# A two-layer decoder step on one core: rectifier and squares regrouped over the engines, and a row spread made with three bf16 pieces

## The chip, the core and the metric

The kernel runs on one core of a Trainium2 chip. The core has a matrix engine (TensorE, PE in the profile; its weight loads are shown apart as PEld), a vector engine (VectorE, DVE), a scalar engine (ScalarE, ACT), a general engine (GpSimd, POOL) and a queue engine that issues transfers (SyncE, SP). The metric is the device time of one execution in microseconds, and the number compared is the median of several executions.

## What is computed

One inference step over 1024 prompt tokens and 32 sample tokens (8 sequences of 4), 1056 columns in all, through two layers. The first layer's mixer is a stabilised matrix-memory recurrence (mLSTM) over 8 heads, evaluated in chunks of 128 tokens; the second's is attention over a paged cache. Both layers end in a squared-ReLU MLP of width 4096. The two pieces that the change touches:

```python
# first mixer, per head and chunk of 128 tokens
b = cumsum(lf); m_inter = b + m
m_t = maximum(m_inter, max(log_d)); w_inter = exp(m_inter - m_t)
s = (q @ k.T) * exp(log_d - m_t)          # log_d = b_t - b_s + ig_s where s <= t
num = w_inter * (q @ C) + s @ v
# MLP, in both layers
u = rmsnorm(h, norm_mlp) @ w_up
h = h + square(relu(u)) @ w_down
```

## The kernel before, in words

Activations lie transposed: features on the partitions, the 1056 tokens as columns, cut into NT = 3 tiles of TW = 352. Every dense product is made of three matmuls on pairs of reduced-precision parts (high by high, high by low, low by high: L212 to L214, and L812 to L814 in the first mixer), so each activation and each weight must exist as a `hi` part and a `lo` part. Weights come in panels of 128 x 1024: SyncE loads one (`w_raw`), GpSimd casts it to `w_hi` (L162) and subtracts to get `w_lo` (L164), and TensorE uses it for three tiles. Two panels are in flight; GpSimd may begin on a buffer once the tiles that read its old contents are done (`tile_ready`). All orders are written out by hand, one program per engine, with counting semaphores between them.

**MLP (`out_and_mlp`).** Eight chunks of 512 hidden features in each layer, 16 in all. A chunk has four `up` panels (u = 0..3), each with three tiles of 24 matmuls, so 12 tiles n = 0..11, and then the `down` product, whose first panel reads, for token tile t, what was made of all four up tiles of t. Each up tile goes through five instructions before `down` can read it: ACT takes it from the accumulator bank with Relu (L2085, which frees the bank, `tile_free`), DVE multiplies by the inverse rms (L2133), ACT squares (L2087), DVE casts the square to `u_hi` (L2135), DVE subtracts `u_hi` from the square to get `u_lo` (L2137, `u_ready`). TensorE's only wait for this, beside the banks, stands at the start of `down` (`u_ready`). The accumulations into `h` in the down part are L2143.

**First mixer (`mixer_a`).** Before the heads can be worked on, a chain on rows of 8 partitions (one per head) x 1056 tokens makes the gate sums `ub` (= b - m, in `squares`) and `winter` (= w_inter), on DVE and ACT in turn, while TensorE makes the first projection tiles; DVE takes those tiles from the banks in the same in-order stream (`read_out`), and TensorE has two banks for them. Then the heads go in four pairs, p = 0..3. For each pair TensorE has to copy a head's row over all 128 partitions. It does so with a small matmul whose stationary operand picks the row: `spread` makes `ub` rows for the decay weights (L850, 512 columns, four per pair, with a bf16 mask added by L852; a small one for the sample tokens at L857), `w_inter` makes `winter` rows for the queries (L866, 352 columns, three per pair, stationary operand `sel`, "p_pair_rows"). Both have f32 operands with 8 rows. The profile shows each such matmul as two records. Between them stand thirds of the next pair's projection tiles, so that TensorE always has work. ACT turns each spread into decay weights (`decay`, L1012, `dec_ready`), and the next spread waits for it since there is one bank. In pairs p > 0 ACT's stream has, between the first and the second decay, the inverse norm of the pair before (`inverse_rms`, L1072 and L1074), which waits for a chain of small DVE instructions (`sums`, L1265 to L1274).

Of the kernel before, what the change touches and what calls it, by code (L numbers as in the profile page):

```python
# [17 lines left out]
ALU = mybir.AluOpType  # L18
# [4 lines left out]
BF16 = mybir.dt.bfloat16  # L23
# [597 lines left out]
def mixer_a(nc, m, own):  # L621
# [7 lines left out]
    FIRST_TILES = 3 * NT + 3  # L629

# [57 lines left out]
    with ExitStack() as c:  # L688
# [13 lines left out]
        pick, sel = sb("pick_gates", [P, P]), sb("pair_rows", [40, HP, P])  # L702
# [4 lines left out]
        graw, y, ub, winter = m.sq[0], m.sq[1], m.acc, m.acc[32:32 + HA, :]  # L707
# [9 lines left out]
        chain, achain, picked = own.sem("dve_step"), own.sem("act_step"), own.sem("gates_picked")  # L717
        y_ready, sp_ready, m_ready, we_in, stack_act = own.sem("softplus_in"), own.sem("softplus_out"), own.sem("m_ready"), own.sem("w_inter_in"), own.sem("stack_act")
# [53 lines left out]
        def _(pool):  # L772
# [17 lines left out]
            heads = m.ident[32:32 + HA, 32:32 + HA].rearrange("r (p h) -> r p h", h=2)  # L790
            pool.tensor_copy(sel[32:32 + HA, :, :].rearrange("r p (h e) -> r p h e", h=2),
                             heads.unsqueeze(3).broadcast_to([HA, HP, 2, DK])).then_inc(filled, 1)
            pool.wait_ge(filled, 12)
# [4 lines left out]
        def _(pe):  # L798
# [43 lines left out]
            def spread(x):  # L842
# [5 lines left out]
                if j < 2:  # L848
                    head = 2 * p + h2
                    pe.matmul(m.bank[2][:, :], m.ident[0:HA, head:head + 1].broadcast_to([HA, P]), ub[0:HA, 512 * j:512 * j + 512],  # L850
                              start=True, stop=False)
                    last = pe.matmul(m.bank[2][:, :], m.identb[:, :], m.causal[:, :].unsqueeze(1).broadcast_to([P, 4, P]),  # L852
                                     start=False, stop=True)
                else:
                    for h2 in range(2):
                        head, z = 2 * p + h2, m.bank[2][0:NS, h2 * NS:(h2 + 1) * NS]
                        pe.matmul(z, m.ident[0:HA, head:head + 1].broadcast_to([HA, NS]), ub[0:HA, SEQ:T], start=True, stop=False)  # L857
# [75 lines left out]
            pe.wait_ge(filled, 12)  # L933
# [16 lines left out]
            pe.wait_ge(col_ready, 5)  # L950
            for p in range(HP + 1):
# [19 lines left out]
        def _(act):  # L971
# [8 lines left out]

            act.wait_ge(y_ready, 1)
# [5 lines left out]
            act.activation(winter, bsum, ACT.Exp).then_inc(stack_act, 1)  # L987
            for g, (b0, nb) in enumerate(GROUPS):
# [123 lines left out]
        def _(dve):  # L1112
# [35 lines left out]
            dve.wait_ge(filled, 12)  # L1148
# [43 lines left out]
            read_out(TAU0 + 5)  # L1192
            dve.wait_ge(stack_act, 2)
# [1055 lines left out]
```

## Time and profile before

| | before |
|---|---|
| median of 3 runs | 3019.81 us (3016.09 to 3023.21) |
| the profiled execution, its own time | 3017.92 us |
| the profiled execution, span of the records | 3016.1 us |
| TensorE matmul busy | 2879.8 us, 95% |
| TensorE weight load busy | 2622.8 us, 87% |
| VectorE busy | 1368.9 us, 45% |
| ScalarE busy | 821.7 us, 27% |
| GpSimd busy | 741.8 us, 25% |
| mean granted TensorE clock | 0.981 of full speed |

The span is the time from the first to the last record of one execution, and what lies around it is 1.8 us. Busy shares are means over stages that differ; how TensorE's idle time and its slots are spent in the two stages in question is in the rows further down. A matmul's own duration includes its way through the array and overlaps with the next: what it takes of TensorE's time is read from the distance of starts.

### The profile page before, as it was taken

The numbers are of one execution on the slowest core, as the hardware profiler recorded it, in microseconds if no ns is written. First come the engines' busy times: TensorE is split into PE (matmuls) and PEld (weight loads), VectorE is DVE, ScalarE is ACT, GpSimd is POOL, SyncE is SP. The second block draws the span as 40 slices with busy tenths as digits, with TensorE's granted clock in tenths as the row PEclk, the third lists the DMA queues.
The fourth block names the chain that finished last, engine by engine and source line by source line (L and its number), as shares of the span: only waits on it lengthen the run. The fifth ranks groups of instructions, "written<-read, shape, count | busy, mean of one in ns | idle before, by whom it ended". The sixth has DMA issues, their size and how long they took to land. (4 is left out here: it accounts for less than half of the span.)

```text
span 3016.1 us, 49373 instructions
## 1 busy us (share of the span) xinstructions
PE 2879.8 (95%) x19749; PEld 2622.8 (87%) x19749; DVE 1368.9 (45%) x2039; ACT 821.7 (27%) x1661; POOL 741.8 (25%) x450
## 2 busy tenths in 40 slices
PE   7999997999999999998999999998799999999998
PEld 6889887999999999996776677665699999999998
DVE  6223345444433344354556655564544443334434
ACT  4121123211110011124555655555321111011112
POOL 3221112223232323232122111210123232323231
PEclk8999998999999999999999999998899999999999
DMA  5575524223232232324443443434311111111112
GB/s 165 182 138 192 99 30 94 84 85 90 91 93 88 85 96 83 98 86 123 116 127 99 120 117 109 123 94 116 127 42 49 43 49 42 44 47 42 49 42 78
DMA packets 361448, 277.24 MB, mean 92 GB/s; under 512 B 31378, under 2 KB 352914, under 8 KB 359250
## 3 DMA queue, kind: packets, MB, share of 16 engines
q1 hardware_dynamic: 340074, 261.97, 29.8%
q10 hardware_dynamic: 21224, 13.15, 2.3%
q8 instruction: 108, 1.77, 0.2%
q14 instruction: 42, 0.34, 0.0%
HBM read 251.06 MB, written 91.11 MB: 113 GB/s over the span
## 5 line engine op out<-in xcount | busy, mean ns | idle before, releaser
L162 POOL CAST w_hi<-w_raw 128x1024 fp32r<-128x1024 f32 x193 | 206.9, 1072 | 1628.1 <-PE bank L214 902.9
L212 PE MATMUL bank<-p_u_hi,w_hi 128*128 128x352 f32 x1536 | 496.8, 323 | 16.0 <-DVE p_u_lo L2137 14.6
L212 PE MATMUL bank<-x_hi,w_hi 128*128 128x352 f32 x1536 | 495.6, 323 | 1.7 <-PEq L2227 1.7
L213 PE MATMUL bank<-p_u_lo,w_hi 128*128 128x352 f32 x1536 | 495.6, 323 | 0.0
L214 PE MATMUL bank<-p_u_hi,w_lo 128*128 128x352 f32 x1536 | 495.4, 323 | 0.0
L214 PE MATMUL bank<-x_hi,w_lo 128*128 128x352 f32 x1536 | 493.5, 321 | 0.0
L213 PE MATMUL bank<-x_lo,w_hi 128*128 128x352 f32 x1536 | 492.9, 321 | 0.0
L164 POOL TENSOR_TENSOR w_lo<-w_raw,w_hi 128x1024 fp32r<-128x1024 f32 x193 | 477.1, 2472 | 15.5
L2143 DVE TENSOR_TENSOR h<-bank,h 128x352 f32<-128x352 f32 x384 | 199.0, 524 | 466.5 <-PE bank L214 466.5
L2085 ACT ACTIVATE p_relu<-bank 128x352 f32<-128x352 f32 x192 | 89.3, 465 | 1039.2 <-PE bank L214 1033.0
L212 PEld LDWEIGHTS bank<-p_u_hi,w_hi 128*128 128x128 f32 x1536 | 288.5, 188 | 20.9 <-issue 18.7
L1886 DVE TENSOR_TENSOR_SCAN square<-square,zero 128x512 f32<-128x512 f32 (+5 forms) x192 | 214.9, 1134 | 167.8 <-ACT square L1746 166.6
L212 PEld LDWEIGHTS bank<-x_hi,w_hi 128*128 128x128 f32 x1536 | 288.1, 188 | 2.8 <-issue 2.8
L213 PEld LDWEIGHTS bank<-x_lo,w_hi 128*128 128x128 f32 x1536 | 289.0, 188 | 0.0
L214 PEld LDWEIGHTS bank<-p_u_hi,w_lo 128*128 128x128 f32 x1536 | 288.7, 188 | 0.0
L213 PEld LDWEIGHTS bank<-p_u_lo,w_hi 128*128 128x128 f32 x1536 | 288.6, 188 | 0.0
L214 PEld LDWEIGHTS bank<-x_hi,w_lo 128*128 128x128 f32 x1536 | 288.4, 188 | 0.0
L2133 DVE TENSOR_TENSOR p_relu<-p_relu,rms_inverse 128x352 f32<-128x352 f32 x192 | 133.3, 694 | 275.4 <-ACT p_relu L2085 275.4
L2135 DVE CAST p_u_hi<-p_relu_sq 128x352 fp32r<-128x352 f32 x192 | 163.2, 850 | 108.4 <-ACT p_relu_sq L2087 108.4
L812 PE MATMUL bank<-x_hi,w_hi 128*128 128x352 f32 x576 | 200.9, 349 | 4.3 <-DVE p_v_next L1138 2.3
L814 PE MATMUL bank<-x_hi,w_lo 128*128 128x352 f32 x576 | 186.8, 324 | 0.0
L813 PE MATMUL bank<-x_lo,w_hi 128*128 128x352 f32 x576 | 186.5, 324 | 0.0
(259 smaller groups left out, 4560.9 us busy)
## 6 DMA issues: line engine op xcount, KB each, us to landing
k_pages<-in_cache_k SPq DMA_DIRECT2D x64, 512.0 KB, 6.2
w_raw<-in_w_up SPq DMA_DIRECT2D x64, 512.0 KB, 4.1
v_pages<-in_cache_v SPq DMA_DIRECT2D x64, 512.0 KB, 4.6
w_raw<-in_w_down SPq DMA_DIRECT2D x64, 512.0 KB, 3.4
p_pages<-k_pages SPq DMA_DIRECT2D x256, 128.0 KB, 2.4
p_pages<-v_pages SPq DMA_DIRECT2D x256, 128.0 KB, 2.4
w_raw<-in_w_in_a SPq DMA_DIRECT2D x25, 512.0 KB, 3.9
h_spill<-h SPq DMA_DIRECT2D x16, 528.0 KB, 5.4
```

The source lines that it names most:

```text
L162: pool.tensor_copy(m.whi[slot][:, :], m.wraw[slot][:, :]).then_inc(w.hi, 1)
L164: pool.tensor_tensor(m.wlo[slot][:, :], m.wraw[slot][:, :], f32(m.whi[slot][:, :]), ALU.subtract)\
L212: pe.matmul(bank[:, 0:TW], wh, xh, start=(k == 0), stop=False)
L213: pe.matmul(bank[:, 0:TW], wh, xl, start=False, stop=False)
L214: last = pe.matmul(bank[:, 0:TW], wl, xh, start=False, stop=(k == nk - 1))
L812: pe.matmul(bank[:, 0:TW], wh, xh, start=(kk == 0), stop=False)
L813: pe.matmul(bank[:, 0:TW], wh, xl, start=False, stop=False)
L814: last = pe.matmul(bank[:, 0:TW], wl, xh, start=False, stop=(kk == KT - 1))
L1886: dve.tensor_tensor_scan(stick, stick, m.zero[:, 0:1].broadcast_to([P, hi - lo]), sticks[h2][:, hi:hi + 1] if x else 1.0, ALU.mult, ALU.ad ...
L2133: dve.tensor_tensor(relu[t][:, :], relu[t][:, :], m.rs[:, toks], ALU.mult).then_inc(scaled, 1)
L2135: dve.tensor_copy(uhi[:, u, toks], sqr[t][:, :]).then_inc(hi_ready, 1)
L2143: dve.tensor_tensor(ht, m.bank[t][:, 0:TW], ht, ALU.add).then_inc(w.tile_free[t], 1)
```

## The change

In the MLP, DVE makes the scaled rectifier in one instruction from the bank (max with 0, times the inverse rms), which now frees the bank. ACT makes both squares from its result, first the one that is written as `u_hi`, then the f32 one. DVE only subtracts. In the first mixer, `ub` and `winter` are each split into three bf16 pieces that add up to the f32 value, at partitions 0, 32 and 64 of a 72-row tensor, and the picking matrices are bf16 with ones at the three places, so that a spread is one bf16 matmul with 72 rows. ACT clears and fills these tensors at the mixer's start, and ACT and DVE make the pieces in turn. GpSimd no longer fills the f32 `sel`.

```diff
+        u3, w3 = own.tensor("u_pieces", [PIECES, T], BF16), own.tensor("w_inter_pieces", [PIECES, T], BF16)
+        of_head, of_pair = own.tensor("head_rows", [PIECES, HA, P], BF16), own.tensor("pair_rows", [PIECES, HP, P], BF16)
...
-                    pe.matmul(m.bank[2][:, :], m.ident[0:HA, head:head + 1].broadcast_to([HA, P]), ub[0:HA, 512 * j:512 * j + 512],
-                              start=True, stop=False)
+                    pe.matmul(m.bank[2][:, :], of_head[:, head, :], u3[:, 512 * j:512 * j + 512], start=True, stop=False)
...
-                pe.matmul(m.bank[7][:, 0:TW], sel[32:32 + HA, p, :], winter[:, x * TW:(x + 1) * TW], start=True, stop=True).then_inc(wsp_ready, 1)
+                pe.matmul(m.bank[7][:, 0:TW], of_pair[:, p, :], w3[:, x * TW:(x + 1) * TW], start=True, stop=True).then_inc(wsp_ready, 1)
...
             pe.wait_ge(col_ready, 5)
+            pe.wait_ge(piece, 4)
+            pe.wait_ge(rest_ready, 4)
...
+            for tile in (u3[:, :], w3[:, :], of_head[:, :, :].rearrange("r h e -> r (h e)"), of_pair[:, :, :].rearrange("r p e -> r (p e)")):
+                step(act.copy(tile, m.zero[0:PIECES, 0:1].broadcast_to([PIECES, tile.shape[-1]])))
+            for r in (0, 32, 64):
+                rows_, heads = slice(r, r + HA), m.identb[r:r + HA, r:r + HA]
+                step(act.copy(of_head[rows_, :, :], heads.unsqueeze(2).broadcast_to([HA, HA, P])))
+                step(act.copy(of_pair[rows_, :, :].rearrange("r p (h e) -> r p h e", h=2),
+                              heads.rearrange("r (p h) -> r p h", h=2).unsqueeze(3).broadcast_to([HA, HP, 2, DK])))
...
+            act.copy(u3[0:HA, :], ub[0:HA, :]).then_inc(piece, 1)
+            act.wait_ge(stack_act, 2)
+            act.copy(w3[32:32 + HA, :], winter).then_inc(piece, 1)
+            act.wait_ge(rest_ready, 1)
+            act.copy(u3[32:32 + HA, :], rest[32:32 + HA, :]).then_inc(piece, 1)
+            act.wait_ge(rest_ready, 2)
+            act.copy(w3[64:64 + HA, :], rest[64:64 + HA, :]).then_inc(piece, 1)
...
             read_out(TAU0 + 5)
+            dve.wait_ge(piece, 1)
+            dve.tensor_tensor(rest[32:32 + HA, :], ub[0:HA, :], u3[0:HA, :], ALU.subtract).then_inc(rest_ready, 1)
             dve.wait_ge(stack_act, 2)
...
             step(dve.memset(num[:, :, :, :], 0.0))
-            for e in range(6, FIRST_TILES):
+            read_out(TAU0 + 6)
+
+            dve.wait_ge(piece, 2)
+            dve.tensor_tensor(rest[64:64 + HA, :], winter, w3[32:32 + HA, :], ALU.subtract).then_inc(rest_ready, 1)
+            dve.wait_ge(piece, 3)
+            dve.wait_ge(rest_ready, 2)
+            dve.tensor_tensor(u3[64:64 + HA, :], rest[32:32 + HA, :], u3[32:32 + HA, :], ALU.subtract).then_inc(rest_ready, 1)
+            read_out(TAU0 + 7)
+            dve.wait_ge(piece, 4)
+            dve.tensor_tensor(w3[0:HA, :], rest[64:64 + HA, :], w3[64:64 + HA, :], ALU.subtract).then_inc(rest_ready, 1)
+            for e in range(8, FIRST_TILES):
                 read_out(TAU0 + e)
...
-                        act.wait_ge(w.tile_ready, i * TILES_C + (TILES_OUT + n + 1))
-                        act.activation(relu[t][:, :], m.bank[t][:, 0:TW], ACT.Relu).then_inc(w.tile_free[t], 1)
-                        act.wait_ge(scaled, i * (UT * NT) + (n + 1))
+                        toks = slice(t * TW, (t + 1) * TW)
+
+                        act.wait_ge(w.tile_free[t], i * USES_C + (USES_OUT + u + 1))
+                        act.activation(uhi[:, u, toks], relu[t][:, :], ACT.Square)
                         act.activation(sqr[t][:, :], relu[t][:, :], ACT.Square).then_inc(sq_ready, 1)
...
-                        dve.wait_ge(w.tile_free[t], i * USES_C + (USES_OUT + u + 1))
-                        dve.tensor_tensor(relu[t][:, :], relu[t][:, :], m.rs[:, toks], ALU.mult).then_inc(scaled, 1)
+                        dve.wait_ge(w.tile_ready, i * TILES_C + (TILES_OUT + n + 1))
+                        dve.scalar_tensor_tensor(out=relu[t][:, :], in0=m.bank[t][:, 0:TW], scalar=0.0, in1=m.rs[:, toks],
+                                                 op0=ALU.max, op1=ALU.mult).then_inc(w.tile_free[t], 1)
                         dve.wait_ge(sq_ready, i * (UT * NT) + (n + 1))
-                        dve.tensor_copy(uhi[:, u, toks], sqr[t][:, :]).then_inc(hi_ready, 1)
-                        dve.wait_ge(hi_ready, i * (UT * NT) + (n + 1))
                         dve.tensor_tensor(ulo[:, u, toks], sqr[t][:, :], f32(uhi[:, u, toks]), ALU.subtract)\
                             .then_inc(u_ready, 1)
```

**The MLP, one up tile.** VectorE's rows for one tile, before (the semaphore that each waits for stands behind it; `relu_scaled` counts DVE's products, `relu_sq_ready` ACT's squares):

```order
L2133 TENSOR_TENSOR p_relu<-p_relu,rms_inverse 128x352 [waits pw1_tile_free0]
L2134 REGISTER_ALU
L2135 CAST p_u_hi<-p_relu_sq 128x352 [waits p3_relu_sq_ready]
L2137 TENSOR_TENSOR p_u_lo<-p_relu_sq,p_u_hi 128x352 [waits p3_u_hi_ready]
```

and now:

```order
L2163 SCALAR_TENSOR_TENSOR p_relu<-bank,rms_inverse 128x352 [waits pw1_tile_ready]
L2165 ISA
L2166 TENSOR_TENSOR p_u_lo<-p_relu_sq,p_u_hi 128x352 [waits p3_relu_sq_ready]
```

VectorE's first instruction now waits for TensorE's tile itself, and the cast is gone from its stream. ScalarE's rows for the same tile were L2085 (Relu from the bank) and L2087 (Square, after `relu_scaled`); now they are two squares side by side:

```order
L2116 ACTIVATE p_u_hi<-p_relu 128x352 [waits pw1_tile_free0]
L2117 ACTIVATE p_relu_sq<-p_relu 128x352
```

**The mixer's start.** VectorE's stream between the projection tiles TAU0+5 and TAU0+8, before (`p_k<-bank` are the read-outs):

```order
L1138 TENSOR_TENSOR p_v_next<-bank,rms_inverse 128x352 [waits pw0_tile_ready]
L1195 COPY p_w_end<-squares 8x8 [waits p2_stack_act]
L1196 COPY p_w_end<-squares 8x8
L1197 TENSOR_TENSOR p_w_diag<-p_w_end,identity 8x128 [waits p2_dve_step]
L1200 MEMSET p_numerator 128x2322
L1136 SCALAR_TENSOR_TENSOR p_k<-bank,rms_inverse 128x352 [waits pw0_tile_ready,p2_dve_step]
L1136 SCALAR_TENSOR_TENSOR p_k<-bank,rms_inverse 128x352 [waits pw0_tile_ready] x2
```

and now:

```order
L1155 TENSOR_TENSOR p_v_next<-bank,rms_inverse 128x352 [waits pw0_tile_ready]
L1211 TENSOR_TENSOR square<-squares,p_u_pieces 8x1056 [waits p2_piece_made]
L1214 COPY p_w_end<-squares 8x8 [waits p2_stack_act]
L1215 COPY p_w_end<-squares 8x8
L1216 TENSOR_TENSOR p_w_diag<-p_w_end,identity 8x128 [waits p2_dve_step]
L1219 MEMSET p_numerator 128x2322
L1153 SCALAR_TENSOR_TENSOR p_k<-bank,rms_inverse 128x352 [waits pw0_tile_ready,p2_dve_step]
L1223 TENSOR_TENSOR square<-squares,p_w_inter_pieces 8x1056 [waits p2_piece_made]
L1226 TENSOR_TENSOR p_u_pieces<-square,p_u_pieces 8x1056 [waits p2_rest_made,p2_piece_made]
L1153 SCALAR_TENSOR_TENSOR p_k<-bank,rms_inverse 128x352 [waits pw0_tile_ready]
L1229 TENSOR_TENSOR p_w_inter_pieces<-square,p_w_inter_pieces 8x1056 [waits p2_piece_made]
L1153 SCALAR_TENSOR_TENSOR p_k<-bank,rms_inverse 128x352 [waits pw0_tile_ready]
```

Four subtractions of 8x1056 have come in between the read-outs. ScalarE's stream has ten fills (L983 to L987) ahead of its first exponential (L982 before) and four casts behind the exponential of `winter` (L987 before). TensorE's stream keeps its order.

## Rows read from the trace of the kernel before

**Rows 1.** The page's slices: granted TensorE clock, in tenths of full speed.

```profile
PEclk8999998999999999999999999998899999999999
```

**Rows 2.** Who waited for whom on TensorE: us in total, times, longest.

```profile
PE bank L212 <- DVE p_u_lo L2137: 14.6, 16, 0.9
```

**Rows 3.** Timeline, the last up tile of an MLP chunk: start, us, engine, instruction, idle before.

```profile
629.68 0.46 ACT L2085 ACTIVATE p_relu<-bank 128x352 f32<-128x352 f32 x1 [2.26 <-PE bank L214]
...
630.93 2.56 POOL L164 TENSOR_TENSOR w_lo<-w_raw,w_hi 128x1024 fp32r<-128x1024 f32 x1
...
631.26 0.50 ACT L2087 ACTIVATE p_relu_sq<-p_relu 128x352 f32<-128x352 f32 x1 [1.11 <-DVE p_relu L2133]
...
631.79 1.89 DVE L2135 CAST p_u_hi<-p_relu_sq 128x352 fp32r<-128x352 f32 x1 [0.56 <-ACT p_relu_sq L2087]
...
633.72 0.53 DVE L2137 TENSOR_TENSOR p_u_lo<-p_relu_sq,p_u_hi 128x352 fp32r<-128x352 f32 x1
...
634.39 0.40 PE L212 MATMUL bank<-p_u_hi,w_hi 128*128 128x352 f32 x1 [0.89 <-DVE p_u_lo L2137]
```

**Rows 4.** The page's group of the additions into h (mean ns after the busy time).

```profile
L2143 DVE TENSOR_TENSOR h<-bank,h 128x352 f32<-128x352 f32 x384 | 199.0, 524 | 466.5 <-PE bank L214 466.5
```

**Rows 5.** Timeline, another up tile: a subtraction beside GpSimd.

```profile
596.59 2.41 POOL L164 TENSOR_TENSOR w_lo<-w_raw,w_hi 128x1024 fp32r<-128x1024 f32 x1
...
596.74 2.64 DVE L2137 TENSOR_TENSOR p_u_lo<-p_relu_sq,p_u_hi 128x352 fp32r<-128x352 f32 x1
```

**Rows 6.** Timeline of TensorE around the first spread of pair 0.

```profile
101.83 0.32 PE L814 MATMUL bank<-x_hi,w_lo 128*128 128x352 f32 x1
...
102.08 1.12 PE L850 MATMUL bank<-squares,identity 8*128 8x512 f32 x2
...
103.14 0.39 PE L852 MATMUL bank<-causal,identity_bf 128*128 128x512 bf16 x1
...
103.53 0.32 PE L813 MATMUL bank<-x_lo,w_hi 128*128 128x352 f32 x1
...
103.69 0.32 PE L814 MATMUL bank<-x_hi,w_lo 128*128 128x352 f32 x1
```

**Rows 7.** Timeline of TensorE around the first query-weight spread of pair 0.

```profile
122.67 0.32 PE L814 MATMUL bank<-x_hi,w_lo 128*128 128x352 f32 x1
...
122.91 0.85 PE L866 MATMUL bank<-squares,p_pair_rows 8*128 8x352 f32 x2
...
123.96 0.32 PE L813 MATMUL bank<-x_lo,w_hi 128*128 128x352 f32 x1
```

**Rows 8.** Timeline, second decay and third spread of pair 1, and of pair 2.

```profile
209.64 1.12 ACT L1012 ACTIVATE p_decay_weights<-bank,p_gate_columns 128x128 f32<-128x128 f32 x4
...
211.11 1.12 PE L850 MATMUL bank<-squares,identity 8*128 8x512 f32 x2
...
311.91 1.13 ACT L1012 ACTIVATE p_decay_weights<-bank,p_gate_columns 128x128 f32<-128x128 f32 x4
...
314.37 1.12 PE L850 MATMUL bank<-squares,identity 8*128 8x512 f32 x2
```

**Rows 9.** Timeline of the mixer's start: ScalarE, VectorE, GpSimd and TensorE.

```profile
59.89 1.08 ACT L982 ACTIVATE p_states<-p_states 8x1056 f32<-8x1056 f32 x1 [13.37 <-DVE p_states L1156]
...
73.80 1.24 DVE L1183 TENSOR_TENSOR p_decay_weights<-p_numerator,p_states 8x1056 f32<-8x1056 f32 x1
...
78.02 1.09 ACT L987 ACTIVATE squares<-p_states 8x1056 f32<-8x1056 f32 x1 [3.88 <-DVE p_states L1189]
...
78.98 2.40 POOL L164 TENSOR_TENSOR w_lo<-w_raw,w_hi 128x1024 fp32r<-128x1024 f32 x1
...
79.14 2.26 DVE L1195 COPY p_w_end<-squares 8x8 f32<-8x8 f32 x1 [0.72 <-ACT squares L987]
...
84.25 0.52 DVE L1136 SCALAR_TENSOR_TENSOR p_k<-bank,rms_inverse 128x352 f32<-128x352 f32 x1
...
85.13 0.32 PE L812 MATMUL bank<-x_hi,w_hi 128*128 128x352 f32 x1
```

More of the change, by code:

```diff
@@ L629, in mixer_a @@
     FIRST_TILES = 3 * NT + 3
+    PIECES = 2 * 32 + HA
     FILL = {"u": 1, "k": 1, "v": 1, "wsp": 2, "out": 1, "scores": 2, "dc": 3, "dcs": 2, "num": 3}
@@ L701, in mixer_a @@
         ss, den, den2 = sb("head_squares", [P, 2, NB]), sb("denominator", [P, 2, NB]), sb("denominator_sq", [P, 2, NB])
-        pick, sel = sb("pick_gates", [P, P]), sb("pair_rows", [40, HP, P])
+        pick = sb("pick_gates", [P, P])
+        u3, w3 = own.tensor("u_pieces", [PIECES, T], BF16), own.tensor("w_inter_pieces", [PIECES, T], BF16)
+        of_head, of_pair = own.tensor("head_rows", [PIECES, HA, P], BF16), own.tensor("pair_rows", [PIECES, HP, P], BF16)
         gbias, m0, mprev, mend = sb("gate_bias", [40, 1]), sb("m_start", [HA, SB]), sb("m_prev", [HA, 16]), sb("m_end", [HA, 16])
@@ L717, in mixer_a @@
         chain, achain, picked = own.sem("dve_step"), own.sem("act_step"), own.sem("gates_picked")
+        piece, rest_ready = own.sem("piece_made"), own.sem("rest_made")
         y_ready, sp_ready, m_ready, we_in, stack_act = own.sem("softplus_in"), own.sem("softplus_out"), own.sem("m_ready"), own.sem("w_inter_in"), own.sem("stack_act")
@@ L789, in _ @@
             pool.wait_ge(filled, 11)
[L790 to L793, printed above, removed]
             weight_splits(pool, m, w, stages)
@@ L856, in spread @@
                         head, z = 2 * p + h2, m.bank[2][0:NS, h2 * NS:(h2 + 1) * NS]
-                        pe.matmul(z, m.ident[0:HA, head:head + 1].broadcast_to([HA, NS]), ub[0:HA, SEQ:T], start=True, stop=False)
+                        pe.matmul(z, of_head[:, head, 0:NS], u3[:, SEQ:T], start=True, stop=False)
                         last = pe.matmul(z, m.identb[0:NS, 0:NS], m.causal_s[:, :], start=False, stop=True)
@@ L932, in _ @@
             pe.wait_ge(w.tile_free[0], NT)
-            pe.wait_ge(filled, 12)
+            pe.wait_ge(filled, 11)
             for t in range(NT):
@@ L1147, in _ @@
             dve.wait_ge(landed, 64)
-            dve.wait_ge(filled, 12)
+            dve.wait_ge(filled, 11)
             dve.wait_ge(picked, NT)
@@ L1961, in out_and_mlp @@
         h_back = [own.sem(f"h_back{k}") for k in range(KT)]
-        scaled, sq_ready, hi_ready, u_ready = own.sem("relu_scaled"), own.sem("relu_sq_ready"), own.sem("u_hi_ready"), own.sem("u_ready")
+        sq_ready, u_ready = own.sem("relu_sq_ready"), own.sem("u_ready")
         out_v = w_out.rearrange("(k p) (m j) -> m p k j", p=P, j=P)
```

2 lines of the change are left out of this document (1 added, 1 removed).

## The prediction

> **What bounds the kernel now.** I read TensorE's waits first, then the timeline of the two stages that the change touches, and last what the other engines do in them. TensorE is busy nearly all the time, so a microsecond is won only where TensorE itself has less to do, or where it stops to wait. In the MLP it stops once a chunk for `u_lo`: 16 times, 14.6 us in all, 0.9 each [rows 2]. The chain behind one such wait is in [rows 3]. The last up tile is ready at 629.68, where ACT begins; DVE's product, ACT's square (631.26), DVE's cast (631.79, 1.89 us) and DVE's subtraction follow, and the subtraction ends at 634.25. TensorE goes on at 634.39, after 0.89 of waiting. The cast is long because of GpSimd: GpSimd's own subtraction runs from 630.93 to 633.49, and the cast ends 0.19 after it. A DVE instruction that has both inputs in SBUF meets the same fate: in [rows 5] a subtraction that began inside GpSimd's ended 0.38 after it (599.38 against 599.00), 2.64 instead of 0.53. Instructions that read a bank don't: the 384 additions into h, many beside GpSimd, have a mean of 524 ns [rows 4].
>
> In the first mixer TensorE hardly waits, it works. One spread there costs it 1.38: from the start of L814 at 101.83 to that of L813 at 103.53 are 1.70, in which two ordinary matmuls take their 0.16 each (103.53 to 103.69) [rows 6]. One query-weight spread costs 0.97 (122.67 to 123.96, less 0.32) [rows 7].
>
> **MLP.** The change takes out ACT's Relu and DVE's cast, puts DVE's one instruction on the bank, and adds a square on ACT. From 629.68: DVE's instruction 0.53 (a scalar_tensor_tensor from a bank took 0.52 [rows 9]; it has one SBUF input and so is like [rows 4]), to 630.21; two squares of 0.50 [rows 3] with 0.04 for each hand-over, to about 631.28. The subtraction can then start, but GpSimd has been at its own since 630.93. So the stall moves from the cast to the subtraction. GpSimd's lasts 2.40 when no cast comes into it (2.41 in [rows 5], 2.40 in [rows 9], against 2.56 in [rows 3]), to 633.33; 0.38 later, at 633.71, `u_lo` is there, 0.54 before the old 634.25. TensorE's wait falls from 0.89 to 0.35. Over 16 chunks: 8.6 us. Bounds: if GpSimd takes 2.56 all the same, 0.38 a chunk, 6.1 us; if the subtraction isn't held at all, the whole wait goes, 14.2 us. I take 8.6, by the row of the same instruction.
>
> The Trainium skill (SBUF — State Buffer, Who interferes with whom) says that the port DVE and GpSimd share is locked for a whole instruction by whoever starts first, and that a DVE instruction with two SBUF inputs contends with a GpSimd one that reads SBUF. This speaks against counting the full 14.2. Taken literally it is a little harsher than the row: the subtraction would run its whole 0.53 after 633.33, to 633.86, which gives 0.39 a chunk and 6.2 us instead of 8.6.
>
> The added square costs nothing: ACT is done at 631.25 and has its next tile 3.8 us (24 matmuls of 0.16) after this one. The bank is freed at 630.21 instead of 630.14, and TensorE needs it two tiles later. DVE's read-outs queue behind the held subtraction as they did behind the held cast, and come out 0.5 earlier.
>
> **Mixer, what TensorE saves.** The bf16 mask matmul of 512 columns takes 0.23 of TensorE's time (103.14 to 103.53, less one slot of 0.16) [rows 6]. The new spread has that form, with 72 rows instead of 128; I give it 0.23, plus the gap of 0.09 that stands ahead of the f32 one (102.08 less 101.83 less 0.16). The f32 one took 1.38 less 0.23, 1.15. Saved: 0.83, 16 times, 13.3 us. The query-weight spread has 352 columns: 0.16 plus 0.09 against 0.97, saved 0.72, 12 times, 8.7 us. Together 22.0. The four small sample spreads I leave out. Bound: four passes of 0.23 are 0.92, and the f32 spread from 102.08 on took 1.06; if the 0.14 of loads and gaps stays with each of the 28, 3.9 less. On the other side there is no more than the 0.09 of each, 2.5.
>
> **Where a part is given back.** There is one bank for the spreads, so the third waits until ACT has read the second out of it. In pair 1 ACT's second decay ends at 210.76 and the third spread begins at 211.11 [rows 8]. ACT can't be earlier: its stream has the inverse norm of the pair before ahead of that decay, and this waits for DVE's chain of sums, which starts with the last projection tile of the pair before, ahead of the first spread. So the third spread can come forward only by 0.35, less 0.14 of hand-over (634.25 to 634.39 in [rows 3]), where the first two have saved 1.66: 1.45 is lost. Pair 3 has the same distances. In pair 2 the decay ends at 313.04 and the spread begins at 314.37, so 1.19 can be used and 0.47 is lost. Pair 0 has no inverse norm. Given back: 3.4.
>
> **The mixer's start.** ACT's ten fills stand ahead of its first exponential. By width (1.08 for 1056 columns [rows 9]) they come to 1.1, 1.1, 1.05, 0.5 and three times 1.6, with hand-overs about 9 us. The exponential now comes at 59.89 after 13.37 of idle time [rows 9], with only two transfer issues in it, so the fills are hidden; were that cover gone, each microsecond would be one later for the projection tiles behind DVE. Taking the fill of `sel` from GpSimd gives nothing, since its first split there waits for a load.
>
> DVE's four subtractions of 8x1056 are 1.24 each [rows 9]. The first waits for ACT's cast (79.11 plus 1.08, 80.2) and so falls into GpSimd's subtraction (78.98 to 81.38). An instruction so held ends its free time, less 0.15, after GpSimd's end (0.38 for 0.53 in [rows 5]), so it ends at 81.38 less 0.15 plus 1.24, 82.5. The copy that stands behind it was held by the same GpSimd instruction and ended at 81.40. All behind it thus comes 1.1 later: the read-out at 84.25, which ended at 84.77, now ends at 85.9, and the tile for which TensorE needs that bank began at 85.13 and now begins at 86.0. Cost 0.9. The next read-out stands behind two more subtractions (to 88.4, read by 88.9), and TensorE is at its tile until 89.8. All pieces are there by about 91, and the first spread begins at 102.08 [rows 6], 11 us later: the new waits of TensorE cost nothing.
>
> **Sum.** 8.6 plus 22.0 less 3.4 less 0.9 is 26.3. The profiled execution took 3017.92, which leaves 2991.6; the median of the runs shown is 1.9 above it, so about 2993.
>
> **The rivals.**
> *The subtraction gets ahead of GpSimd* (chance 0.12). Then the 0.89 goes whole, 14.2 for 8.6: 2988. It would have to start 0.35 earlier than I find.
> *The third spreads are not held* (0.08). If the chain of sums moves forward with TensorE after all, 3.4 come back: 2990. Against it stands that DVE's chain begins before the first spread.
> *Smaller terms* (0.17). The 0.14 stays with each spread and the MLP gives 6.2: 6.3 less, 3000. What speaks for it is that 72 rows and a changed stationary operand occur in no row.
> *A late start* (0.08). The fills, at four thirds of their price, 12 us, would just fit; if the pieces' exchange or the fills push the first tiles by 3 to 6 us more, 2996 to 3000.
> *The mixer gains nothing* (0.02), since TensorE's gain is all taken by other waits: 8.6 alone, 3011.
> *The clock falls: slower than before* (0.03). The granted clock is the thing that could undo it all. Slices of 75.4 us stand at 8 tenths, which is a part of the slice at 1.2 instead of 2.4 GHz, the others at 9 or more [rows 1]; one such slice costs up to 0.2 times 75.4, 15 us. From two more of them (30 against 26.3) it decides, and the time would be about 3024. The new pauses at the mixer's start (0.9) and at two third spreads (1.5) could do it. Against it: the 16 waits of 0.9 in the MLP left the slices at 9.
> The forecast itself has 0.50.
>
> **How the numbers follow.** The range reaches from the full MLP gain with the 3.5 us by which the runs shown scatter, 2985, to the smaller terms, 3001. It leaves out the dead mixer, the falling clock and the tails of the others, some 0.15. A measurement of this kernel can tell about 0.2%, 6 us. All cases but the last lie more than that below 3019.81, so faster has 0.96, the same 0.01, slower 0.03.
>
> **What would show it.** The wait of L212's successor for `u_lo` at 16 times 0.35, 5 to 6 us in all; the subtraction in the last up tiles at 2.3 to 2.5 us and no longer 0.53, GpSimd's beside it at 2.40; no DVE cast. The spread at one record of about 0.4 and 0.55 from neighbour to neighbour with the mask; a wait or gap of 1.4 ahead of the third spread of pairs 1 and 3; the first read-out of `k` about 1.1 later against its tile. I am wrong if the subtraction has 0.53 there, if the 72-row matmul is slow, or if the clock's slices show new eights.

## The result, and the profile after

The changed kernel takes 2979.27 us (median of 4 runs, 2977.72 to 2984.09), beside 3017.95 (3015.16 to 3023.21) for the kernel before: ratio 0.9878, 95% interval [0.9861, 0.9894]. The forecast was 2993, with a range down to 2985: right in sign and close in the two stages that it took apart, 12 us too little in all. The profiled execution took 2977.9 us.

The page of the changed kernel, busy time and the granted clock by slices:

```profile
PE 2847.8 (96%) x19713; PEld 2609.5 (88%) x19713; DVE 1303.7 (44%) x1851; ACT 819.4 (28%) x1675; POOL 731.6 (25%) x449
...
PEclk9999998999999999999999999999899999999999
```

TensorE has 36 records fewer (19749 before), and two slices fewer at 8 tenths than in [rows 1].

**MLP.** The timeline around the last up tile of a chunk (start, us, engine, instruction, idle before), and the wait's row of the waits of TensorE:

```profile
610.95 0.53 DVE L2163 SCALAR_TENSOR_TENSOR p_relu<-bank,rms_inverse 128x352 f32<-128x352 f32 x1 [1.81 <-PE bank L214]
...
611.51 0.50 ACT L2116 ACTIVATE p_u_hi<-p_relu 128x352 fp32r<-128x352 f32 x1 [2.93 <-DVE p_relu L2163]
...
611.91 0.48 ACT L2117 ACTIVATE p_relu_sq<-p_relu 128x352 f32<-128x352 f32 x1
...
612.20 2.40 POOL L164 TENSOR_TENSOR w_lo<-w_raw,w_hi 128x1024 fp32r<-128x1024 f32 x1
...
612.43 2.55 DVE L2166 TENSOR_TENSOR p_u_lo<-p_relu_sq,p_u_hi 128x352 fp32r<-128x352 f32 x1 [0.95 <-ACT p_relu_sq L2117]
...
614.44 0.32 PE L214 MATMUL bank<-p_u_hi,w_lo 128*128 128x352 f32 x1
...
615.13 0.40 PE L212 MATMUL bank<-p_u_hi,w_hi 128*128 128x352 f32 x1 [0.36 <-DVE p_u_lo L2166]
615.37 0.32 PE L213 MATMUL bank<-p_u_lo,w_hi 128*128 128x352 f32 x1
```

```profile
PE bank L212 <- DVE p_u_lo L2166: 5.8, 16, 0.4
```

This is the picture of [rows 3] with one engine's turn less. GpSimd takes its undisturbed 2.40; the subtraction that began 0.23 later lasts 2.55 instead of 0.53 and ends at 614.98, 0.38 after GpSimd. The wait is 0.36, where [rows 2] have 0.9.

**First mixer.** A spread with its mask, and a query-weight spread, each with a neighbour:

```profile
102.75 0.32 PE L814 MATMUL bank<-x_hi,w_lo 128*128 128x352 f32 x1
102.91 0.39 PE L850 MATMUL bank<-p_u_pieces,p_head_rows 72*128 72x512 bf16 x1
103.14 0.38 PE L851 MATMUL bank<-causal,identity_bf 128*128 128x512 bf16 x1
103.17 0.51 PE L812 MATMUL bank<-x_hi,w_hi 128*128 128x352 f32 x1
103.52 0.32 PE L813 MATMUL bank<-x_lo,w_hi 128*128 128x352 f32 x1
...
120.06 0.32 PE L814 MATMUL bank<-x_hi,w_lo 128*128 128x352 f32 x1
120.22 0.32 PE L865 MATMUL bank<-p_w_inter_pieces,p_pair_rows 72*128 72x352 bf16 x1
120.26 0.45 PE L812 MATMUL bank<-x_hi,w_hi 128*128 128x352 f32 x1
120.54 0.32 PE L813 MATMUL bank<-x_lo,w_hi 128*128 128x352 f32 x1
```

From L814 to L813 are 0.77 less two slots of 0.16: 0.45 for a spread and its mask, for 1.38 in [rows 6]. The other costs 0.48 less 0.32, 0.16, for 0.97 in [rows 7]. The pair of small sample spreads went the other way: with their masks they cost 0.67 (116.55 to 117.54, less 0.32) for 0.48 before (119.34 to 120.14), four times, 0.8 us in all. What is given back: the third spread of pair 1 (timeline), and TensorE's waits in the first mixer:

```profile
204.13 0.31 ACT L1089 ACTIVATE p_head_squares<-p_head_squares,eps 128x18 f32<-128x18 f32 x1 [3.92 <-DVE p_head_squares L1303]
...
204.60 1.12 ACT L1029 ACTIVATE p_decay_weights<-bank,p_gate_columns 128x128 f32<-128x128 f32 x4
...
205.78 0.39 PE L850 MATMUL bank<-p_u_pieces,p_head_rows 72*128 72x512 bf16 x1 [1.46 <-ACT p_decay_weights L1029]
```

```profile
PE bank L850 <- ACT p_decay_weights L1029: 3.5, 3, 1.5
PE bank L812 <- DVE p_k L1153: 0.9, 1, 0.9
```

The first of these rows holds three waits: 1.46 in pair 1 and 1.46 in pair 3, each of the third spread for the second decay, and 0.56 in pair 2. The one in pair 2 is another: there the second spread waits for the first decay, which comes late behind four output transfers that ScalarE issues (ACTq) and a table load:

```profile
298.75 0.61 ACTq L1124 DMA_DIRECT2D out_n_sample<-p_state_sample  x1
299.46 1.14 ACT L1029 ACTIVATE p_decay_weights<-bank,p_gate_columns 128x128 f32<-128x128 f32 x4 [0.19 <-issue]
...
300.65 0.39 PE L850 MATMUL bank<-p_u_pieces,p_head_rows 72*128 72x512 bf16 x1 [0.56 <-ACT p_decay_weights L1029]
```

**By stages.** The view of windows for the changed kernel: stretch, its us, busy time of each engine (instructions), granted clock, share of the DMA engines, GB/s. The stretches are first mixer, first MLP, second mixer, second MLP with the end:

```profile
45.60:464.90 419.30, 395.37 (x2769) 359.34 (x2769) 163.10 (x303) 97.03 (x205) 95.41 (x61) 0.97 0.53 123
...
571.50:1319.60 748.10, 743.81 (x4634) 740.27 (x4634) 284.80 (x401) 104.31 (x213) 227.26 (x130) 1.00 0.30 92
1319.60:2113.10 793.50, 730.25 (x6278) 542.10 (x6277) 444.15 (x602) 436.28 (x916) 127.81 (x71) 0.98 0.40 113
...
2219.80:2976.10 756.30, 742.05 (x4640) 736.95 (x4638) 275.32 (x412) 100.22 (x247) 213.17 (x124) 1.00 0.16 48
```

In the profile of the kernel before, the same stages take 438.9, 752.4, 805.9 and 761.0 us. The two that were changed are 28.6 us shorter together (19.6, 4.3, 4.7). The second mixer, in whose program no line was touched, is 12.4 us shorter, and this is what the forecast lacks. How much of it is the change and how much is scatter, the experiments have to tell.

### The profile page after: what moved, and what is told of

It reads as the page before. It is cut to its first block and busy times, and to the rows that moved or that the text cites. A ratio compares the mean times of both kernels' runs of the same rounds, so it can differ in the third digit from the quotient of the medians.

```text
span 2976.1 us, 49009 instructions
## 1 busy us (share of the span) xinstructions
PE 2847.8 (96%) x19713; PEld 2609.5 (88%) x19713; DVE 1303.7 (44%) x1851; ACT 819.4 (28%) x1675; POOL 731.6 (25%) x449
## 5 line engine op out<-in xcount | busy, mean ns | idle before, releaser
L164 POOL TENSOR_TENSOR w_lo<-w_raw,w_hi 128x1024 fp32r<-128x1024 f32 x193 | 468.2, 2426 | 15.5
L2116 ACT ACTIVATE p_u_hi<-p_relu 128x352 fp32r<-128x352 f32 x192 | 95.7, 499 | 1207.0 <-DVE p_relu L2163 1207.0
L2166 DVE TENSOR_TENSOR p_u_lo<-p_relu_sq,p_u_hi 128x352 fp32r<-128x352 f32 x192 | 229.1, 1193 | 182.7 <-ACT p_relu_sq L2117 182.7
L2163 DVE SCALAR_TENSOR_TENSOR p_relu<-bank,rms_inverse 128x352 f32<-128x352 f32 x192 | 100.0, 521 | 270.9 <-PE bank L214 263.5
L814 PE MATMUL bank<-x_hi,w_lo 128*128 128x352 f32 x576 | 186.3, 323 | 0.0
L813 PE MATMUL bank<-x_lo,w_hi 128*128 128x352 f32 x576 | 186.1, 323 | 0.0
```

Source lines behind the costliest of these rows:

```text
L164: pool.tensor_tensor(m.wlo[slot][:, :], m.wraw[slot][:, :], f32(m.whi[slot][:, :]), ALU.subtract)\
L813: pe.matmul(bank[:, 0:TW], wh, xl, start=False, stop=False)
L814: last = pe.matmul(bank[:, 0:TW], wl, xh, start=False, stop=(kk == KT - 1))
L2163: dve.scalar_tensor_tensor(out=relu[t][:, :], in0=m.bank[t][:, 0:TW], scalar=0.0, in1=m.rs[:, toks], op0=ALU.max, op1=ALU.mult).then_inc(w ...
L2166: dve.tensor_tensor(ulo[:, u, toks], sqr[t][:, :], f32(uhi[:, u, toks]), ALU.subtract)\
```

## The experiments

All ratios are to the kernel before, run beside each.

**One part alone, and both kernels again.** The first has the diff's part in `out_and_mlp` alone, the second its part in `mixer_a` alone:

```diff
 # e1: only this half of the change
+dve.scalar_tensor_tensor(out=relu[t][:, :], in0=m.bank[t][:, 0:TW], scalar=0.0, in1=m.rs[:, toks], ...)
 # e2: only this half of the change
+pe.matmul(m.bank[2][:, :], of_head[:, head, :], u3[:, 512 * j:512 * j + 512], start=True, stop=False)
```

> Only the MLP part of the change. Theory A (the MLP gives its shorter wait, 16 times 0.53 us, and nothing else): 8.6 us less than before, 0.9971; the second mixer takes its 808 us as before. Theory B (a faster MLP also moves the second mixer to fewer stretches at the lower clock, which is where the 12 us beyond the prediction lie): 8.6 plus some 6 to 12, 15 to 21 us less, 0.993 to 0.995.

> Only the first mixer's part of the change. Theory A (the direct gain alone): 18.7 us less than before, 0.9938. Theory B (the 12 us in the second mixer come with this part): 25 to 31 us less, 0.990 to 0.992, and fewer stretches at half clock between the two MLPs. Theory C (chance): the second mixer's time differs from execution to execution of the same kernel by up to 12 us, so that this kernel's runs scatter by that much.

> The kernel before, unchanged, a second profile of it. Theory C (chance): its second mixer takes another time than 808 us, and its waits for the value pages are not those of the first profile (2 us each, with half clock in the same places). Theories A and B: 808 us within 2 and the same stretches at half clock.

> The changed kernel, unchanged, a second profile of it. Theory C (chance): a second mixer of up to 808 us in some executions, and a time of up to 2990. Theories A and B: 796 us within 2, 2979 in all.

Measured: MLP alone 3011.01, 0.9973 [0.9961, 0.9984], which is 8.1 us by the ratio and 6.1 by the medians; mixer alone 2988.87, 0.9909 [0.9894, 0.9925]; before again 1.0001 [0.9989, 1.0013]; after again 2986.05, 0.9893 [0.9877, 0.9909]. With the MLP's part alone the second mixer keeps its 803.3 us, with the first mixer's alone it has 792.6. So the extra comes with the first mixer's part. It also scatters: the changed kernel again had 799.7 there, and the kernel before again 802.2 for 805.9.

**Where the second mixer waits.** TensorE's waits in it, of the kernel before (e3, from 1345 to 2135 us) and of the changed kernel (from 1325 to 2100 us):

```profile
PE bank L1673 <- DMA p_pages<-v_pages: 13.2, 10, 2.3
```

```profile
PE bank L1702 <- DMA p_pages<-v_pages: 8.8, 9, 2.3
```

Apart from the stage's own start the other rows of the two differ by 0.7 us or less. The waits are for pages of values, for the last of four quarters of their products, and they stand at other places: about 61, 254, 446, 641 and 740 us into the stage before, 158, 350, 542 and 771 after (these places are counted from 2.2 us behind the start of the stretches above). The stage works through eight pairs of heads. The pattern has a period of two pairs (193 us) and has moved by one pair. What has such a period? The DMA view of the second mixer (e3) shows it:

```profile
q1 hardware_dynamic: 182832, 88.39, 38.9%
q8 instruction: 52, 0.85, 0.4%
q14 instruction: 21, 0.17, 0.1%
```

A queue carries instructions in packets of 16 KB, 52 in a stage of 6278 matmuls: one per 121. Eight pairs share 52 packets, so a pair takes 6.5, and two pairs a whole number. The 36 records that the change took away are 0.3 of a packet, an estimate from 72 instructions of 256 in one. The Trainium skill (Runtime: NRT & Kernel Launch, Instruction fetch mechanics) says the instruction memory is refilled in 16 KiB blocks of 256 instructions; with a weight load and a matmul for each record that is 128, less the other instructions, and the trace agrees. It also calls the cost "mostly hidden". The next runs ask whether it is.

**The packets moved by small matmuls.** One edit with four sizes, N = 36, 128, 64 in the changed kernel and 92 in the kernel before, at the head of TensorE's program of the second mixer:

```diff
+            for _ in range(N):
+                pe.matmul(m.bank[2][0:32, 0:32], m.identb[:, 0:32], m.identb[:, 0:32], start=True, stop=True)
             for e in range(NT, TILES):
```

> The changed kernel with 36 small matmuls (32x32, bf16, into a bank that is free then) at the head of TensorE's program of the second mixer; nothing else is changed. The change took 36 matmul records out of the first mixer (19749 to 19713), each a weight load and a matmul in the instruction stream, and the DMA queue that carries instructions moves TensorE's stream in packets of 16 KB, one per about 124 matmuls in the second mixer; in the kernel before, every long wait for a value page began 3.3 to 3.7 us after such a packet, in the changed kernel the waits are at other places, 4.6 to 5.3 us after one. Theory A (where the packets fall among the page loads sets the waits): with the 36 put back the long waits return to the places of before (about 61, 256, 450, 644, 742 us into the stage, 1.6 to 2.2 us each, with the clock at half level there), the second mixer takes 799 to 806 us instead of 793, and the whole 6 to 12 us more than the changed kernel, 2986 to 2992. Rival B (the second mixer got shorter for another reason, for one the lighter load of GpSimd's or VectorE's port, or the moment at which it starts): the waits stay at 158, 350, 542 us, and the time is the changed kernel's plus about 1 us for the matmuls, 2979 to 2986.

> The same with 128 small matmuls, 256 instructions of 64 bytes, which is one packet of 16 KB: Theory A: the packets fall where they fall in the changed kernel, so the waits stay at about 158, 350, 542 and 771 us into the stage, 1 to 1.5 us each, and the time is the changed kernel's plus the 128 matmuls themselves (at the least 128 x 0.03 = 4 us if nothing hides them). The 36 of the run beside it then cost more in the stage than these 128 do, but for that issue. Theory C (any matmuls added there disturb the stage): more waits and more half clock than with 36.

> The same with 64 small matmuls, 128 instructions, half a packet. A pair takes 6.5 packets (the pattern repeats every two pairs), so half a packet moves the pattern by one pair. Theory A: short waits (1 to 1.5 us) as in the changed kernel, but one pair (97 us) off: at about 61, 256, 450, 644 us into the stage and not at 158, 350, 542; time as the changed kernel's plus 2 us. Rival B: waits stay at 158, 350, 542.

> The kernel before with 92 small matmuls at the same place: 184 instructions forward, which is 72 back from the next packet's start, where the changed kernel stands. Theory A: long waits at the places of before are gone, the waits are short and at about 158, 350, 542 us into the stage, the second mixer takes 793 to 797 us beside 802 to 806, half clock there about 36 us beside 52 to 60, and the whole 4 to 10 us less the 92 matmuls' 3 us: 3009 to 3017 beside 3017. Rival B: waits as in the kernel before, and 3 us more: 3020.

Measured, with two earlier runs. The waits listed are those of 1.25 us and more behind the stage's start. The distance is, at the first of them, from the point where the DMA view lists the packet to the end of the wait (the texts above have it 0.8 us larger, and where they say that a wait began, its end is meant):

| kernel | us | ratio | waits for value pages, us into the stage | packet ahead by |
|---|---|---|---|---|
| before (e3) | 3016.55 | 1.0001 [0.9989, 1.0013] | 61, 254, 446, 641, 739, 779 | 2.5 |
| after, N = 36 (e5) | 2990.29 | 0.9917 [0.9903, 0.9930] | 61, 254, 446, 735, 775 | 2.7 |
| after (e4) | 2986.05 | 0.9893 [0.9877, 0.9909] | 158, 350, 542, 774 | 4.4 |
| after, N = 128 (e6) | 2983.11 | 0.9885 [0.9870, 0.9900] | 160, 352, 544, 777 | 4.3 |
| before, N = 92 (e8) | 3012.22 | 0.9986 [0.9977, 0.9996] | 160, 352, 544, 775 | 4.3 |
| after, N = 64 (e7) | 2986.98 | 0.9899 [0.9884, 0.9914] | 62, 254, 446, 641, 738, 777 | 4.6 |

Two of the waits, each as the timeline and as the DMA view of one microsecond has it. The changed kernel with N = 36, DMA view from 1381 to 1382:

```profile
1383.95 0.64 PE L1702 MATMUL bank<-p_pages,p_weights_sample_t 128*32 128x128 f32 x16 [2.04 <-DMA p_pages<-v_pages]
```

```profile
q1 hardware_dynamic: 353, 0.17, 63.5%
q8 instruction: 1, 0.02, 7.9%
```

The changed kernel itself (e12, below), DMA view from 1474 to 1475:

```profile
1479.06 0.64 PE L1702 MATMUL bank<-p_pages,p_weights_sample_t 128*32 128x128 f32 x16 [1.48 <-DMA p_pages<-v_pages]
```

```profile
q8 instruction: 1, 0.02, 5.8%
```

7.9% of 16 engines for 1 us is 1.26 us of one engine. That a packet of page data which needs the same engine has to stand back for so long is argued and not shown: the view does not say which engine carried what. What is shown is that the places follow the packets in all four cases, whichever kernel it is: 36 put the changed kernel's waits where the kernel before has them, a whole packet leaves them, half a packet moves them by one pair, and 92 give the kernel before the places of the changed one. For the places, rival B is out. And the wait at the end of a pair goes with the distance. Over the traces with this order of the products, the stage's last wait left out, it was 1.6 to 2.5 us with a packet 2.2 to 3.1 us ahead of its end, 1.0 to 2.0 with one 3.8 to 5.0 ahead, 0.3 to 0.8 with one 5.6 to 6.3 ahead. Counted from the start of the wait, the packet comes 0.7 us ahead at one pair of the kernel before (e3) and 5.6 at the next; in the changed kernel (e4) it comes 2.6 us later, so the 5.6 becomes 3.0 (the new wait of 1.4) and the 0.7 falls behind the wait (which shrinks from 1.8 to 0.5).

The price is less sure than the places. By the medians N = 36 against 128 is 7.2 us, and the 128 themselves take 3.4 us (1322.4 to 1325.8) where the 36 take 0.9, so 9.7. But N = 64 stands as well as N = 128, and against it, with its own 1.7 us taken off, the price is 4.1. N = 92 gains 4.0 against the kernel before on the same chip and takes 2.4 itself, so 6.4. The profiled executions of these four don't show the price at all: the second mixer takes 799.9 us with 36, 803.0 with 128, 799.7 with 64 and 801.2 with 92, and with the small matmuls taken off all four lie between 798.0 and 799.6 (the profiled execution with 36, 2983.57 us, is also the fastest of its five). It takes all traces with this order to see it: the five with the packets near (before, before again, MLP alone, N = 36, e16) have a mean of 803.5 us in the second mixer, small matmuls taken off, 799.0 to 807.2; the ten others 797.6, 792.5 to 799.8. That is 5.9 us, with waits for value pages of 12.4 us for 9.9.

With 36, that is with the packets where they were, the change is worth 25.9 us by the medians (3016.20 to 2990.29), with an interval from 21 to 29.

**The two waits that the change left, one edit each.** And both, and the changed kernel beside them.

```diff
 # e9, ScalarE's program of the first mixer
-                    if i == 1 and p:
+                    if i == 2 and p:
                         inverse_rms(p - 1)
 # e10, MLP
-                        act.activation(sqr[t][:, :], relu[t][:, :], ACT.Square).then_inc(sq_ready, 1)
+                        act.activation(m.bank[3 + t][:, 0:TW], relu[t][:, :], ACT.Square).then_inc(sq_ready, 1)
...
-                        dve.tensor_tensor(ulo[:, u, toks], sqr[t][:, :], f32(uhi[:, u, toks]), ALU.subtract)\
+                        dve.tensor_tensor(ulo[:, u, toks], m.bank[3 + t][:, 0:TW], f32(uhi[:, u, toks]), ALU.subtract)\
```

> The changed kernel with ScalarE's inverse mean square of the heads of the pair before (L1089, L1091) put behind the second decay of a pair and no longer ahead of it. In the changed kernel the third spread of pairs 1 to 3 waits 1.5 us each for that decay (bank L850 <- ACT p_decay_weights L1029: 3.5 us in 3), since ScalarE first waits 3.9 us for VectorE's head squares (ACT L1089 204.13). Theory (that wait is what became late when the spreads got short, and it is on the path): the three waits go, the first mixer takes 3.5 us less, 416 beside 419.5, and the whole 0.9988 of the changed kernel. Rival (VectorE's norm then comes later and the turns of the outputs wait for it, or the third decay becomes late instead): the first mixer unchanged within 1 us, with new waits at the turns.

> The changed kernel with the MLP's f32 square written by ScalarE into a free bank and not into an SBUF tile, so that VectorE's subtraction reads one operand from SBUF and one from PSUM. In the changed kernel 62 of its 192 subtractions take 2.55 us and not 0.53, each beside a product of GpSimd's, and the first down tile of a block waits 0.36 us for the last of them, 16 times (5.8 us); none of the 192 scaled rectifiers, which read one operand from PSUM and one from SBUF, takes over 0.53 us. Theory (GpSimd holds a VectorE operation only where both its inputs are in SBUF): the 62 long ones are gone, the wait of 5.8 us too, the MLP stages take 2.9 us less each and the whole 5 to 6 us. Rival (any VectorE operation that begins under GpSimd's is held, and the rectifiers only escape by their moment): subtractions of 2.5 us remain and the time is the changed kernel's within 1 us.

> Both edits, the inverse mean square later and the square in a bank: by the theories of the two runs beside it their gains add, 9 us less than the changed kernel: 2971 to 2977.

> The changed kernel itself once more, on the chip of the three runs beside it, as what they are read against: 2979 to 2986, and the waits for value pages in the second mixer again at about 158, 350, 542 and 771 us into the stage.

Measured: e9 2980.34, 0.9875 [0.9859, 0.9890]; e10 2972.66, 0.9858 [0.9841, 0.9875]; e11 2969.79, 0.9839 [0.9823, 0.9855]; e12 2984.07, 0.9890 [0.9875, 0.9905]. Both together are 14.3 us below the changed kernel beside them, more than the 9 expected; by stages they are 2.8 and 9.9, 12.7. In e9 the waits of pairs 1 and 3 are gone and the one of pair 2 stays, since it has nothing to do with the inverse norm:

```profile
PE bank L850 <- ACT p_decay_weights L1029: 1.1, 1, 1.1
```

and the first mixer takes 417.4 for 420.2, 2.8 us less (3.5 expected); the whole can't tell e9 from e12, their intervals overlap. In e10 (the subtraction's row by source line: shortest, median and longest in ns) none is held:

```profile
L2166 DVE TENSOR_TENSOR p_u_lo<-bank,p_u_hi x192: 523/525/527, 576.7 to 2904.7; 128x352 fp32r<-128x352 f32 x192
```

TensorE's wait for `u_lo` is gone, and the MLP stages take 743.1 and 751.5 for 748.2 and 756.3: 9.9 us, not the 5.8 of the wait. The rows of the changed kernel's MLP say why. From the last matmul ahead of the wait to the second one behind it are 614.44 to 615.37, 0.93, where two slots take 0.32. So a chunk loses 0.61, of which the view of waits names 0.36: the rest is the overlap of one matmul with the next, which a pause breaks. 16 times 0.61 is 9.8.

**The last quarter later.** In the second mixer, TensorE's order only:

```diff
                 if tiles:
                     z(p, n, 0)
+                while held:
+                    values(*held.pop(0))
...
-                for y in quarters[placed:]:
-                    values(*y)
+                held.extend(quarters[placed:])
```

> The changed kernel with the last quarter of a half pair's value products (L1702) put behind the first scores of the next slot (L1592, 1.2 us of matmuls) in TensorE's order of the second mixer; the same work, one step later, and no loads moved. Every wait for a value page in the second mixer is one of this last quarter: SyncE issues its eight loads in 6.6 us and the last lands 2.6 us after its issue. Theory A (an instruction packet among these loads makes the last one late, TensorE waits 1.3 to 2.9 us, and its clock falls at some of these waits): the waits for value pages at 158, 350, 542 us go or fall below 0.5 us, and the second mixer takes 4 to 8 us less than the 793 to 800 of the changed kernel; whole 2974 to 2980. Rival D (the loads of the key pages that follow wait for the same buffers, so the time is lost one step on): waits for key pages (L1623) of about the same size come up 3 us later, the time the same.

> The same order with the 36 small matmuls at the stage's head, which put the packets back to where they fall in the kernel before. Theory A, if the step later gives the loads enough time: the position of the packets no longer matters, and the time is that of the run beside it within 2 us (36 small matmuls take 0.9 us); with the old order the 36 cost about 8 us. If the slack of 1.2 us is too short for a packet 3.4 us ahead of the wait: waits of 0.4 to 0.9 us come up at 61, 254, 446 us and 3 to 5 us are lost. Rival (the position acts in another way than through these waits): the full 8 us between the two.

> The same order together with the two edits that gained 12 to 14 us in the first mixer and the MLP (inverse mean square later, square in a bank): by theory A these add, 2961 to 2967; by rival D 2969 to 2973, as the two edits alone.

> The two edits alone (2969.8) with the 36 small matmuls at the head of the second mixer: the effect of the packets' position once more, on a kernel whose other stages are shorter. Theory A: waits at about 61, 254, 446, 641 us and 5 to 9 us more, 2975 to 2979. If the 8 us between the runs with 36 and 128 were scatter: 2970 to 2972.

Measured: e13 2971.82, 0.9848 [0.9832, 0.9865]; e14 2977.98, 0.9863 [0.9848, 0.9879]; e15 2960.05, 0.9809 [0.9794, 0.9823]; e16 2978.83, 0.9866 [0.9850, 0.9882]. TensorE's waits in the second mixer for the value pages, e13 and then e14:

```profile
PE bank L1702 <- DMA p_pages<-v_pages: 3.8, 4, 1.5
```

```profile
PE bank L1702 <- DMA p_pages<-v_pages: 7.6, 6, 1.7
```

The later quarter takes away most of the waits, no wait for key pages takes their place (the one of 3.0 us at the stage's start was there before; rival D is out), and the second mixer falls to 786.0 us, more than expected. In e14 the outcome named for too short a slack came: the packets that come 2.4 to 2.9 us ahead still go with waits of 0.9 to 1.7, and 6.2 us are lost, of which 0.9 are the small matmuls, both somewhat more than that text says; the intervals of the two overlap. e16 repeats the effect of the position with the old order: 9.0 us more than e11, which ran on another chip (8.1 by the ratios, whose intervals overlap a little), with waits of 2.0 to 2.5 at 63, 258, 455, 649 us. The version with all three edits, e15, is the fastest: 58 us below the kernel before.

What a wait costs beyond itself is the clock. In the kernel before, each of the five waits for value pages of 1.6 us or more has a stretch at 1.2 GHz, 3.4 or 6.8 us long, that begins less than 2 us behind its end; in the changed kernel only one of the four of 1.3 to 2.3 us has (3.4). Summed over the records of the granted clock, to 2 us behind the stage's end, the second mixer's time at 1.2 GHz and its length go together:

| | e13 | after | e11 | e12 | e5 | e8 | after again | e7 | before again | e6 | e16 | before |
|---|---|---|---|---|---|---|---|---|---|---|---|---|
| us at 1.2 instead of 2.4 GHz | 24.8 | 35.5 | 40.0 | 40.7 | 46.2 | 48.4 | 48.5 | 49.0 | 52.1 | 52.3 | 56.0 | 60.0 |
| second mixer, us | 786.0 | 793.5 | 798.5 | 797.6 | 799.9 | 801.2 | 799.7 | 799.7 | 802.2 | 803.0 | 808.1 | 805.9 |

From e13 to e16 the waits grow by 10.2 us (3.8 to 14.0) and the time at the lower level by 31.2, which at half speed is at most 15.6: together they bound the 22.1 us between the two. Three profiles of one and the same kernel have 35.5, 40.7 and 48.5, with the waits at the same places. Why the clock falls at a wait in one execution and not in the next is open.

## Why the prediction was right, and where it was not

- **MLP, 8.6 forecast: right.** The stall moved to the subtraction, which ends 0.38 after GpSimd, GpSimd takes 2.40, TensorE waits 0.36 (0.35 forecast), and the two stages gave 4.3 and 4.7. The rule of the Trainium skill (SBUF — State Buffer, Who interferes with whom) taken to the letter gave 6.2; the subtraction ended 0.38 and not 0.53 after GpSimd, and the measurement decides. The same section says that a VectorE instruction with one SBUF input doesn't contend; e10 agrees, 192 of 192 at 0.53.
- **Mixer, what TensorE saves, 22.0 forecast: the mechanism right, the size too small.** The slots are 0.45 and 0.16, not 0.55 and 0.25: the gap of 0.09 that was carried over from the f32 row doesn't stand ahead of a bf16 matmul, even with 72 rows and another stationary operand. 16 times 0.93 and 12 times 0.81 are 24.6. The bound "no more than the 0.09 of each, 2.5" was the truth. The sample spreads, left out (as four; they are eight), cost 0.8 more. 24.6 less 0.8, 3.5 and 0.9 are 19.4; the stage gave 19.6, and the forecast for it was 17.7.
- **Given back, 3.4: right for pairs 1 and 3, by luck for pair 2.** The third spreads of pairs 1 and 3 wait 1.46 each (1.45 forecast), behind the inverse norm of the pair before, and e9 shows that it is ScalarE's order: both waits go with it. In pair 2 the forecast had 0.47 at the third spread; that one doesn't wait, and the 0.56 that is there belongs to the second, behind a first decay that comes late after ScalarE's output transfers. The total of 3.5 agrees because the two happen to be alike.
- **The mixer's start, 0.9: right,** 0.86, behind a VectorE subtraction of 2.25 us (80.00 to 82.25) that GpSimd held; the fills are hidden.
- **The sum: this is the step that failed.** It took all stages but two as they were, and so put the second mixer at nothing without giving a reason; that stage was 12.4 us shorter in the first comparison. The rivals had the clock falling, at new pauses of the changed stages; none had it rise, and none let the first mixer's code reach the second mixer. The change shortened TensorE's instruction stream by 36 records, and the 16 KB packets of the second mixer moved against its page loads: its waits for value pages went to other places and became shorter (12.8 to 8.8 us), and its clock fell less often. The runs with moved packets show this for the places; the price that they give is 4 to 10 us by medians, and 5.9 over all traces. So of the 12.4 us that the first two profiles differ by there, about half is the packets and the rest is scatter. The 19.6 and 9.0 of the changed stages and the 5.9 make 34.5, an estimate; the three comparisons of the changed kernel gave 38.7, 31.0 and 33.5, with a mean of 34.4. The first of them, against which the forecast stands, was the largest; with the packets put back (e5) the change is worth 25.9, forecast 26.3, which is closer than the scatter allows one to expect.

## What to carry to other kernels

When a program with unrolled code waits for a load that is issued just in time, its time can also hang on where the instruction packets fall: before a difference of a few tenths of a per cent is put down to an edit, look at the stages that the edit did not touch, and move the packets with a few idle instructions as a control; and take more than one profile of each, since here single ones did not show what the medians did. The lasting remedy is slack: one step between the last load and its use gave more here than either position. And an intermediate that VectorE reads with a second operand from SBUF is better left in a bank when GpSimd is busy on the same stretch.

## What the runs showed of the hardware

- An instruction packet of 16 KB takes one DMA engine about 1 us (median 1.04; four in five between 0.92 and 1.34), and one comes per 121 matmuls in the second mixer. How long TensorE waited for a value page at the end of a pair of heads, in the order of before, went with its distance: 1.6 to 2.5 us where it lay 2.2 to 3.1 us ahead of the end of the wait, 1.0 to 2.0 where it lay 3.8 to 5.0 ahead, 0.3 to 0.8 where it lay 5.6 to 6.3 ahead.
- The pause of TensorE at the start of `down` costs 0.25 us more than the idle time that is shown for it (0.61 for 0.36; before the change 1.15 for 0.91). Ahead of a bf16 spread it is 0.16 more (1.62 for 1.46).
- A spread of 512 columns takes about 0.22 us of TensorE's time with 72 rows in bf16 (0.45 with its mask, which takes 0.23), and took 1.15 with 8 rows in f32 (1.38 with the mask).
- ScalarE's square of 352 columns took 0.45 us into a bank (e10) and 0.48 into SBUF. The Trainium skill (ScalarE: Activation LUTs, Step-by-step: what each stage is for) says that PSUM is the lower-latency destination; the rows agree.
